# Rotary sums moved to VectorE, query transposes moved into the key block, and a sample's own scores split over two groups

## What is computed

```
h = RMSNorm(x) * (1 + scale) + shift
zq, zkv, zd, ga, gb, ma, mb = split(h @ w_in)       # zq 384 wide, zkv 256+32, zd 3 groups x (q|k|v) x 256
q    = rms(zq, qa_norm) @ w_qb                      # 8 heads x 96
rows = [rms(zkv[:256]), rope(rms(zkv[256:]))]       # latent key rows
dq, dk = rope(rms(zd q)), rope(rms(zd k))           # 3 dilated groups, 4 heads x 64
rope(x) = [x1*cos - x2*sin, x2*cos + x1*sin]
a = latent attention(q, rows)                       # prompt; samples read a paged cache of 4096 rows
b = dilated window attention(dq, dk, dv), 3 groups combined
y = x + gate * ((sigmoid(ma)*((a*silu(ga))@w_pa) + sigmoid(mb)*((b*silu(gb))@w_pb)) @ w_out)
```

## Time and profile before

| what | value |
|---|---|
| three timed runs | 1233.58, 1255.19, 1259.21 us; median 1255.19 |
| the profiled execution | 1232.98 us, span 1231.1 us |
| PE matmul busy | 1106.2 us (90%), 8538 instructions |
| DVE busy | 696.1 us (57%), 1611 |
| ACT busy | 506.6 us (41%), 1226 |
| POOL busy | 251.8 us (20%), 264 |
| granted TensorE clock, mean | 0.957 of full speed |

### The profile page before, as it was taken

How to read it: one execution, slowest core, us unless ns; L and a number is a source line. 1 busy time by engine, 2 the same in 40 slices (tenths; PEclk the granted TensorE clock), 3 DMA queues, 4 the chain that set the end, 5 groups by cost and what they waited for, 6 DMA issues and landing times.

```text
span 1231.1 us, 24990 instructions
## 1 busy us (share of the span) xinstructions
PE 1106.2 (90%) x8538; PEld 946.0 (77%) x8538; DVE 696.1 (57%) x1611; ACT 506.6 (41%) x1226; POOL 251.8 (20%) x264
## 2 busy tenths in 40 slices
PE   4697899998898999999988999998999899998987
PEld 2596777876676777777768989988898898988863
DVE  4526867585545451310365676766576666767661
...
GB/s 327 254 66 75 18 64 5 10 78 56 69 113 107 48 55 84 120 69 103 143 184 156 108 116 45 92 76 93 70 92 79 93 89 63 94 74 92 79 113 81
DMA packets 82013, 115.53 MB, mean 94 GB/s; under 512 B 8907, under 2 KB 57180, under 8 KB 81901
## 3 DMA queue, kind: packets, MB, share of 16 engines
...
...
## 4 chain that ended last, share of the span: by engine, by line
PE 60%; DVE 15%; issue 10%; POOL 6%; ACT 6%; DMA 2%; DVEq 0%; SPq 0%; ACTq 0%; POOLq 0%
PE ps L1523 18%; PE ps L1178 7%; PE ps L1180 6%; PE ps L1179 6%; PE ps L1504 5%; DVE ssq L2387 3%; PE ps L1549 3%; ACT cT_hi L960 2%; PE ps L1327 2%; PE ps L1170 2%; POOL wlo L1038 1%; PE ps L1321 1%; POOL tmp L1053 1%; DMA wuk_raw<-in_w_uk 1%; PE ps L1607 1%
## 5 line engine op out<-in xcount | busy, mean ns | idle before, releaser
L1038 POOL TENSOR_TENSOR wlo<-raw,whi 128x512 fp32r<-128x512 f32 (+3 forms) x148 | 168.7, 1145 | 363.7 <-ACT whi L682 363.4
L1523 PE MATMUL ps<-wq_hi,cT_hi 128*128 128x260 f32 x1024 | 219.4, 296 | 1.7 <-issue 1.5
L1178 PE MATMUL ps<-whi,hT_hi 128*128 128x512 f32 (+3 forms) x512 | 195.4, 382 | 25.4 <-POOL wlo L1038 20.6
L1523 PE MATMUL ps<-wq_hi,cT_lo 128*128 128x260 f32 x1024 | 207.7, 284 | 0.0
L1523 PE MATMUL ps<-wq_lo,cT_hi 128*128 128x260 f32 x1024 | 207.5, 284 | 0.0
L2387 DVE TENSOR_REDUCE ssq<-sq 128x8 f32<-128x512 f32 x256 | 172.2, 682 | 59.3 <-ACT sq L991 52.5
L682 ACT ACTIVATE whi<-raw 128x512 fp32r<-128x512 f32 (+3 forms) x148 | 82.9, 563 | 291.2 <-PE ps L1180 124.8
L1180 PE MATMUL ps<-whi,hT_lo 128*128 128x512 f32 (+3 forms) x512 | 187.1, 366 | 0.0
L1179 PE MATMUL ps<-wlo,hT_hi 128*128 128x512 f32 (+3 forms) x512 | 187.0, 365 | 0.0
L1523 PEld LDWEIGHTS ps<-wq_hi,cT_hi 128*128 128x128 f32 x1024 | 159.6, 192 | 2.1 <-issue 1.7
L1523 PEld LDWEIGHTS ps<-wq_lo,cT_hi 128*128 128x128 f32 x1024 | 159.7, 191 | 0.0
...
## 6 DMA issues: line engine op xcount, KB each, us to landing
cn<-in_cache_mla SPq DMA_DIRECT2D x256, 144.0 KB, 2.1
...
```

Source lines behind the costliest of these rows:

```text
L1038: nc.gpsimd.tensor_tensor(out=wlo[:, s % NHL, 0:width], in0=raw[:, SLOT[j], 0:width], in1=whi[:, s % NHL, 0:width].bitcast(F32), op=ALU.su ...
L1178: mm(out, hi[:, k, c], bh, start=st, stop=False)
L1523: last = mm(ps[:, 3 + 2 * (u % 2) + f, 0:260], a[c], wq[:, c, f, w], start=c == 0 and a is hi and wq is wq_hi, stop=c == 1 and a is lo)
```

## The change

Three edits.

1. In the dilated step the two sums of a tile leave POOL and go to DVE, in a new function `rotated(g, t)`. DVE does those of tile t-1 after it has written y of tile t, and those of the samples behind the copy of the samples' values. The semaphore `y_roped` is replaced by `y_ready`, `cos_done` and `sin_done`. POOL makes two more `wlo` pieces at the end of a group, ahead of its store of the window.
2. The three Tq items are numbered between Q and KV. PE transposes them ahead of pieces 5, 6 and 7 of block KV; ACT writes each high half when it has split up to that piece, and splits the next piece after it. Two items get other banks: the samples' KV item takes the bank of Q's first tile, and the third Tq item that of the first Tq.
3. In the last batch the product and the sums of the samples' own scores stand at (0, 2) and (0, 3), and `window_maxima` at (1, 1).

```diff
@@ -101,7 +101,7 @@
 
 STAGES = ([("ada0", 1, "A"), ("ada1", 1, "A"), ("wukT", 2, "A"), ("xT", KD, "A")]
           + [(f"ada{n}", 1, "A") for n in range(2, 6)]
-          + [("Q", 5, "A"), ("KV", 5, "A"), ("Tq", 3, "D"), ("QB0", 5, "A"),
+          + [("Q", 5, "A"), ("Tq", 3, "D"), ("KV", 5, "A"), ("QB0", 5, "A"),
              ("Tr", 2, "D"), ("K", 5, "A"), ("V", 4, "A"), ("QB1", 5, "A"), ("TkM", 8, "A"), ("D0QK", 5, "A"), ("TqM", 8, "A")])
 for _g in range(ND):
     STAGES += [(f"D{_g}QK", 5, "A"), (f"D{_g}V", 5, "A")][_g == 0:]
@@ -147,6 +147,9 @@
 SHARES_BANK = [ITEM["GB"], ITEM["GB"] + 2]
 HELD_BY = {ITEM["GB"] + t: ITEM["GA"] - 2 + t // 2 for t in range(NT)}
 HELD_BY[ITEM["GBs"]] = None
+_tq, _kv = ITEM["Tq"], ITEM["KV"] + NT
+PLACE[_kv], HELD_BY[_kv], HELD_BY[_tq + 2 + BANKS] = (ITEM["Q"] % BANKS, 0), ITEM["Q"], _kv
+PLACE[_tq + 2], HELD_BY[_tq + 2], HELD_BY[_kv + BANKS] = (_tq % BANKS, 0), _tq, _tq + 2
 for _t in range(4):
     PLACE[ITEM["TE"] + _t], HELD_BY[ITEM["TE"] + _t] = (_ga[_t], 0), ITEM["GA"] + _t
 
@@ -452,7 +455,7 @@
         smp_ready = sem("smp_ready")
         squared, square_free, kc_rope, qh1_pool = (
             sem("squared"), sem("square_free"), sem("kc_rope"), sem("qh1_pool"))
-        y_roped, rope_done = sem("y_roped"), sem("rope_done")
+        y_ready, sin_done, cos_done, rope_done = sem("y_ready"), sem("sin_done"), sem("cos_done"), sem("rope_done")
         qk_done, masked, exp_done, tr_done, trp_done, pt_a, pt_d, pv_chunk, o_done = (
             sem("qk_done"), sem("masked"), sem("exp_done"), sem("tr_done"), sem("trp_done"), sem("pt_a"),
             sem("pt_d"), sem("pv_chunk"), sem("o_done"))
@@ -812,13 +815,17 @@
             for n in range(4, 6):
                 to_stage_rows(ITEM[f"ada{n}"], 512, NB + 1)
 
-            for name, w in (("Q", QR), ("KV", CW)):
-                split_for(name)
-                for t in range(NT):
-                    to_stage(ITEM[name] + t, w)
-                to_stage_rows(ITEM[name] + TS, w)
+            split_for("Q")
+            for t in range(NT):
+                to_stage(ITEM["Q"] + t, QR)
+            to_stage_rows(ITEM["Q"] + TS, QR)
             for c in range(3):
+                split_to(FIRST["KV"] + (6, 7, 8)[c])
                 half(ITEM["Tq"] + c, qaThi[:, c, :], scale=colt[:, KD + c:KD + c + 1])
+            split_for("KV")
+            for t in range(NT):
+                to_stage(ITEM["KV"] + t, CW)
+            to_stage_rows(ITEM["KV"] + TS, CW)
 
             def stage_q(i):
                 split_for(f"QB{i}")
@@ -1043,22 +1050,14 @@
 
                 n = lanes(t)
                 y = tmp[0:n, c % 2, :].rearrange("p (h e) -> p h e", e=DH)
-                t1 = tmp[0:n, 2, :]
                 t2 = tmp[0:n, 3, :].rearrange("p (h e) -> p h e", e=DH)
                 sin = ropes[0:n, t, 64:128]
-                pool.wait_ge(y_roped, 2 * c + 1)
+                pool.wait_ge(y_ready, c + 1)
                 if c:
                     pool.wait_ge(rope_done, c)
                 nc.gpsimd.tensor_tensor(out=t2[:, :, 0:32], in0=y[:, :, 32:64], in1=rep(sin[:, 0:32], 1, 8), op=ALU.mult)
-                link(nc.gpsimd.tensor_tensor(out=t2[:, :, 32:64], in0=y[:, :, 0:32], in1=rep(sin[:, 32:64], 1, 8),
-                                             op=ALU.mult))
-                pool.wait_ge(y_roped, 2 * c + 2)
-                q_out = dq_s[:, g, :] if t == TS else dqn[:, g, t, :]
-                k_out = kv_s[:, g, 0:BW] if t == TS else kvo[:, g, t, 0:BW]
-                t2f = tmp[0:n, 3, :]
-                nc.gpsimd.tensor_tensor(out=q_out, in0=t1[:, 0:BW], in1=t2f[:, 0:BW], op=ALU.add)
-                nc.gpsimd.tensor_tensor(out=k_out, in0=t1[:, BW:2 * BW], in1=t2f[:, BW:2 * BW], op=ALU.add)\
-                  .then_inc(rope_done, 1)
+                nc.gpsimd.tensor_tensor(out=t2[:, :, 32:64], in0=y[:, :, 0:32], in1=rep(sin[:, 32:64], 1, 8),
+                                        op=ALU.mult).then_inc(sin_done, 1)
 
             nc.gpsimd.memset(cs, 0.0)
             nc.gpsimd.memset(ones[:, :], 1.0).then_inc(zeroed, 1)
@@ -1103,6 +1102,7 @@
                 for t in range(5):
                     rotate(g, t, 5 * g + t)
                     low_to(low[0] + 1)
+                low_to(low[0] + 2)
                 wait_evac(pool, ITEM[f"D{g}V"] + NT - 1)
                 pool.wait_ge(rope_done, 5 * g + 5)
                 if g == 0:
@@ -1231,12 +1231,17 @@
             for n in range(4, 6):
                 block_direct(f"ada{n}", cs)
 
-            for name in ("Q", "KV"):
-                block_of(name, ITEM[name], range(5), hThi, hTlo, hTs, wait_h=name == "Q")
-            pe.wait_ge(qan_ready, 1)
-            for c in range(3):
-                transposes(ITEM["Tq"] + c, [(t * P, P, qan[:, t, c * P:(c + 1) * P]) for t in range(NT)])
-            misc_transposes([(NB * c, P, qan[0:NB, TS, c * P:(c + 1) * P]) for c in range(3)], NB)
+            def turned_queries(k):
+                if k == 5:
+                    pe.wait_ge(qan_ready, 1)
+                if k in (5, 6, 7):
+                    c = k - 5
+                    transposes(ITEM["Tq"] + c, [(t * P, P, qan[:, t, c * P:(c + 1) * P]) for t in range(NT)])
+                if k == 7:
+                    misc_transposes([(NB * c, P, qan[0:NB, TS, c * P:(c + 1) * P]) for c in range(3)], NB)
+
+            block_of("Q", ITEM["Q"], range(5), hThi, hTlo, hTs, wait_h=True)
+            block_of("KV", ITEM["KV"], range(5), hThi, hTlo, hTs, ahead_of=turned_queries)
             wait_evac(pe, ITEM["Tq"] + 2)
             pe.wait_ge(smp_ready, SMP_Q)
             block_of("QB0", ITEM["QB0"], range(5), qaThi, qaTlo, qaTs)
@@ -1748,7 +1753,7 @@
             def low_half(idx, out, hi, scale=None):
 
                 dve.wait_ge(act_half, HALF_NO[idx])
-                src = ps[:, idx % BANKS, :]
+                src = ps[:, place(idx)[0], :]
                 if scale is None:
                     ins = v.tensor_tensor(out=out, in0=src, in1=hi.bitcast(F32), op=ALU.subtract)
                 else:
@@ -2036,6 +2041,19 @@
             link(v.tensor_tensor(out=snew[:, :].rearrange("p (b h) -> p b h", b=NB), in0=rep(dns[:, :], 1, NB),
                                  in1=rep(newmask, 2, HM), op=ALU.add))
 
+            def rotated(g, t):
+
+                c, n = 5 * g + t, lanes(t)
+                t1, t2 = tmp[0:n, 2, :], tmp[0:n, 3, :]
+                q_out = dq_s[:, g, :] if t == TS else dqn[:, g, t, :]
+                k_out = kv_s[:, g, 0:BW] if t == TS else kvo[:, g, t, 0:BW]
+                dve.wait_ge(cos_done, c + 1)
+                dve.wait_ge(sin_done, c + 1)
+                v.tensor_tensor(out=q_out, in0=t1[:, 0:BW], in1=t2[:, 0:BW], op=ALU.add)
+                v.tensor_tensor(out=k_out, in0=t1[:, BW:2 * BW], in1=t2[:, BW:2 * BW], op=ALU.add)\
+                 .then_inc(rope_done, 1)
+                dve.wait_ge(rope_done, c + 1)
+
             for g in range(ND):
                 zs = [head_squares(f"D{g}QK", t) for t in range(5)]
                 inv_rms(40, 1.0 / DH)
@@ -2044,24 +2062,25 @@
                     n, z3 = lanes(t), zs[t]
                     y = tmp[0:n, c % 2, :]
                     if c >= 2:
-                        dve.wait_ge(rope_done, c - 1)
+                        dve.wait_ge(sin_done, c - 1)
                     free_stage(v.tensor_tensor(out=y.rearrange("p (h e) -> p h e", e=DH), in0=z3,
                                                in1=rep(rsy[0:n, 8 * t:8 * t + 8], 2, DH), op=ALU.mult))
                     for m, o in enumerate((G_DQ, G_DK)):
                         yh = y[:, m * BW:(m + 1) * BW].rearrange("p (h e) -> p h e", e=DH)
                         last = v.tensor_tensor(out=yh, in0=yh, in1=rep(gn[0:n, o + g * DH:o + (g + 1) * DH], 1, HD),
                                                op=ALU.mult)
-                    last.then_inc(y_roped, 1)
-                    dve.wait_ge(y_roped, 2 * c + 1)
-                    if c >= 1:
-                        dve.wait_ge(rope_done, c)
+                    last.then_inc(y_ready, 1)
+                    dve.wait_ge(y_ready, c + 1)
+                    if t:
+                        rotated(g, t - 1)
                     v.tensor_tensor(out=tmp[0:n, 2, :].rearrange("p (h e) -> p h e", e=DH),
                                     in0=y.rearrange("p (h e) -> p h e", e=DH),
-                                    in1=rep(ropes[0:n, t, 0:64], 1, 2 * HD), op=ALU.mult).then_inc(y_roped, 1)
+                                    in1=rep(ropes[0:n, t, 0:64], 1, 2 * HD), op=ALU.mult).then_inc(cos_done, 1)
                 wait_evac(dve, ITEM[f"D{g}V"] + TS)
                 z = stage[0:NB, staged[0] % NSTAGE, 0:BW]
                 staged[0] += 1
                 free_stage(v.tensor_copy(kv_s[:, g, BW:2 * BW], z))
+                rotated(g, TS)
             dve.wait_ge(rope_done, 5 * ND)
             v.memset(flag[:, :], 0.0).then_inc(smp_ready, 1)
 
@@ -2246,6 +2265,9 @@
```

(5 more changed lines are left out.)

## The result

The changed kernel took 1226.86 us (median of 8 runs, 1223.31 to 1246.79), the kernel before 1235.91 in the same sitting (8 runs, 1229.08 to 1259.21). The ratio is 0.9949 with a 95% interval of 0.9926 to 0.9973: 0.51% faster (0.27 to 0.74), that is 6.3 us. The profiled execution took 1227.17 us, its span is 1224.6, its mean granted clock 0.960.

The account below looks back on a forecast made before the run. It took PE to wait for POOL and DVE, whose instructions run one after another in the dilated step, and for DVE in the query step and last batch; 7.6 + 1.1 + 0.8 = 9.5 us, giving 1245.5, range 1216 to 1256.

Parts of the forecast that it names:

- The time as stated, 1245.5: Whole kernel: the median of the three runs shown, 1255.19, times 0.9923; 1223.5 for an execution like the profiled one.
- The turn of the loop: Dilated step, from one `wlo` to the next on POOL: 4.98 us in place of 5.27, 0.29 less a turn.
- the order adds a wait: Dilated step: POOL's next sin products wait for DVE's sums to free tmp 3, 1.15 us behind `wlo`.
- The bound of 4.70: Dilated step: pure sum of POOL's and DVE's work in a turn, 4.70 us, with DVE's sums at 0.29 each.
- The three groups: Dilated step: last `wlo` of D1QK 2.5 us sooner, of D2QK 3.0; in group 2, 2.1 of POOL's 2.8 come through.
- The two `wlo` ahead of the store: End of a group, ahead of POOL's window store: they cost nothing; without that cover 1.4 us a group.
- The transposes in KV: Query and key step: DVE begins KV's squares near 102.25 in place of 103.33, 1.1 us less.
- The rival: Query step gives nothing or costs: pieces 5 to 7 at 1.2 GHz, squares 4 late; 1228.6 or 1250.7; chance 0.13.
- The last batch: `window_maxima` leaves DVE's work ahead of the `s_rotary` copy: 0.8 us off PE's stand of 3.98.
- The sum: Whole kernel: 7.6 + 1.1 + 0.8 = 9.5 us saved, 0.77%.
- Everything behind these three pieces starts from them: After the dilated step's three last `wlo` pieces: their 7.6 us saving carries through to all later work.
- Its rivals on the clock, one faster and one slower: Shorter stands keep PE at 2.4 GHz, 13 to 18 saved, 0.13; KV pieces 5 to 7 at 1.2 GHz, 4 late, 0.13.

Follow-up runs that it names:

- e_two: The changed kernel with POOL's product with sin going to tmp 3 and tmp 4 in turn; ratio to the kernel before 0.9928 (0.9902 to 0.9954).

## Why the prediction was right and wrong

**The time as stated, 1245.5, was wrong**, and with before at 1230 to 1236 it reads as a loss. The step that failed is "Since a new median can fall on either of these, I give the second as the time". It took the median of three runs, 1255.19, for the kernel's level. More runs put the level at 1230.45 (median of the 56 executions above; 1234.2 is the median of all 95 timed runs of before), near the profiled execution that the whole sum was made against; by their times, two of the three were runs with the long stretch at the low clock. The text had the number 1223.5 for an execution like the profiled one, 3.4 from the median measured and inside the range 1216 to 1256. Three runs that disagree by 2%, of which only one agrees with the trace, don't give a level; here the trace's own time did, 1232.98.

**The turn of the loop**: forecast 4.98, measured 4.94 to 4.99. That the engines form one queue was right, and so was the number, but not its reason, "the order adds a wait": without the wait for tmp 3 the turn stays (e_two, 4.97 and 4.92). The number came out because the path through tmp 3 priced the sums and a gain product of DVE at what they take there. The bound of 4.70 was wrong: it priced DVE's instructions at 0.29 wherever they stand, but 0.29 fits only behind a POOL instruction; behind another of DVE they take 0.38. With this order the sum itself is 4.95.

**The three groups**: forecast 2.5, 3.0 and 2.1. By the means of three traces each, 49.27 to 46.40 and 47.64 to 44.61: 2.9 and 3.0. For the third, 290.39 to 288.95: 1.4, with traces between -0.2 and 2.7; POOL's own 2.9 is sure, what of it comes through isn't. The two `wlo` ahead of the store cost nothing visible. Not foreseen: DVE's copy of the samples' values stands 3.43 us beside three `wlo`,

```profile
281.46 3.43 DVE L2082 COPY kv_s<-stage 8x256 f32<-8x256 f32 x1
```

and so the samples' sums end at 286.1. POOL's store of the window waits 1.20 us for them, at no visible cost, since POOL's next `wlo` then still waits 1.06 for ACT.

**The transposes in KV**: forecast 1.1, measured 0.9 where the clock holds and -0.4 where it falls. Relative to a start 0.74 later, ACT's read-out of KV (101.7 in the text, 101.99), the squares (102.25, 102.41) and QB0's second tile (103.85, 104.11) came some 0.5 us sooner than forecast; the first square then ran 0.6 longer beside `wlo`. The rival was right in kind and priced too high, since 3.4 us at the start of KV and not pieces 5 to 7 ran slow. The 1.61 us of standing for a bank were not forecast as such.

**The last batch**: 0.8 forecast and 0.8 measured, in every trace with the third edit (3.16 to 3.18 in place of 3.98).

**The sum.** 9.5 forecast; up to the tail 9.8 by the means of three traces (1115.56 to 1105.77 from the read-out of Q to `esm`). That is in part luck: 1.1 of it lie between the rows and loop 1, where no edit is, and more than make up for the third loop. What failed is the step from there to the time: "Everything behind these three pieces starts from them". The traces then give 2.4 back in the tail and 0.6 ahead of Q, and over all runs 5.0 us of the 9.5 are left (6.3 in the first comparison). Lengths outside the edits move by up to 7 us from one execution to the next, so 0.77% as a forecast of time needed a discount that the text didn't make: an interval of its own for PE's clock in the parts not touched, in both directions. Its rivals on the clock, one faster and one slower, stand only in the places that it touches.
